# Turns of the probabilities moved directly behind the scores in two attentions of a one-core transformer kernel

## The chip, the cores and the metric

The kernel runs on one core of a Trainium2 chip. The metric is device time in microseconds (us). Three runs of the kernel before took 1641.87, 1641.92 and 1642.34 us, median 1641.92 us.

## The reference

The program computes two model blocks on one sequence of 512 tokens with width 1024, all in float32. Of these two places matter here.

The first is the attention of the first block (called **A** here): 8 heads of 64, chunks of 64 queries, each sees its own chunk and up to eight chunks to the left, with a relative bias.

```
sc = jnp.einsum('bqhd,bkhd->bhqk', q_blk, kb).astype(jnp.float32) * scale + bias
sc = jnp.where(valid[None, None, None, :], sc, -1e30)
pr = jax.nn.softmax(sc, axis=-1).astype(vb.dtype)
return jnp.einsum('bhqk,bkhd->bqhd', pr, vb)
```

The second is the sparse attention of the second block (**D** here): 8 query heads in 2 groups, and for each query block three softmaxes (over compressed keys, over selected blocks, over a window), whose outputs are weighted by gates and added:

```
o_c = jnp.einsum('bgrqn,bgnd->bgrqd', p_c, v_cmp)
o_s = jnp.einsum('bgrqn,bgqnd->bgrqd', p_s, vs_g)
o_w = jnp.einsum('bgrqn,bgnd->bgrqd', p_w, vwb)
return g_blk[..., 0:1] * o_c + g_blk[..., 1:2] * o_s + g_blk[..., 2:3] * o_w
```

Before, between and behind them stand the projections, a short convolution, a mixture of experts (96 matrices of 2 MB, streamed), an mLSTM and an HGRN layer.

## The kernel before

Every engine has one instruction stream, written out by hand in program order: `tensor` (TensorE), `vector` (VectorE), `scalar` (ScalarE), `gpsimd` and `sync` (which issues the weight DMAs). The streams meet at semaphores only. A PSUM bank is a `Fill`: TensorE waits in `fill` until the reader of the bank's previous contents has freed it (`pe.wait_ge(f.free, f.before)`), and the readers wait for `f.full`.

Both attentions are software pipelines over items. An item is a pair of heads (`hh`, u = 0 and 1) and one or two query tiles ("parts"), with at most 512 columns of scores for each head. `ITEMS_A` has 12 items (3 for each head pair), `ITEMS` has 24 (6 for each pair: one of `kind` 0 for the compressed keys, five others). The first of the five has one part, the second also, the other three have two.

In step i, TensorE does these, in this order (`softmax_a`, `softmax_d`):

1. `score(i)`: the scores of both heads, 64 rows each, in two banks of a ring of three.
2. `filling(2 * i)`: pieces of other work, to fill the time in which the other engines work on the softmax. In A a piece is a part of a projection (`seventh`, 4 matmuls, 8 in the trace, since each float32 matmul stands there twice); in D it is a part of the output projection of the mLSTM half (`out_part`, 2 matmuls, 4 in the trace).
3. `turn_probs(i - 2)`: the probabilities of item i-2 are transposed on TensorE, one bank for each head. **The ring of the turns has two banks**, `Ring(banks[3:5])`. So the first head's turns wait for the copy of the first head of item i-3, and the second head's for that of the second.
4. `filling(2 * i + 1)`.
5. `values(i - 3)`: probabilities times values.

The other engines do in step i: VectorE `lows(i)` (scores plus bias or mask, and their maximum, with a `ttr` for each part and head), `weigh(i - 1)` behind an item of kind 0, its own share of the pieces of `filling(2 * i)`, then `probs(i - 2)`, the copy of the first head's turns from PSUM, then its share of `filling(2 * i + 1)`. ScalarE does `act(..., ACT.Exp)` for each part and head of item i, and behind them `probs(i - 2)` for the second head. GpSimd scales the probabilities by the reciprocal of their sum (`weigh_a`, `weigh_d`); it signals "pa" or "pd" once for each head, and the turns wait for that.

The pieces are dealt out at build time by `softmax_slots` into two slots for each step: 4.76 pieces a step in A (2 or 3 in each slot), 0.81 in D. In D the slots `2 * i` that hold a piece, with a turn in the same step, are those of steps 2, 6, 7, 11, 12, 16, 17, 22 and 23; steps 5, 10, 15, 21, 25 and 26 hold none in either slot.

Of the kernel before, what the change touches and what calls it, by code (L numbers as in the profile page):

```python
# [186 lines left out]
def build(nc, T, out):  # L187
    with ExitStack() as ctx:
# [259 lines left out]
        ITEMS_A = list(items_a())  # L448
        NIA = len(ITEMS_A)
        ITEMS = list(items_d())  # L450
        NIT = len(ITEMS)
# [14 lines left out]
        def tensor(pe):  # L466
# [159 lines left out]
            def softmax_a(piece):  # L626
                scores, turns, out_, filler = Ring(banks[0:3]), Ring(banks[3:5]), Ring(banks[5:6]), Ring(banks[6:])

                def filling(slot):
                    now[0] = filler  # L630
                    for g, p in FILL_A[slot]:
                        piece(g, p)

                def score(it):
                    now[0] = scores
                    for u in range(2):
                        fill(("sa", it["x"] + u))
                    for part in it["parts"]:
                        c, q, nk = part["o"], part["q"], part["nk"]
                        for u in range(2):  # L640
                            f, o = F["sa", it["x"] + u], slice(64 * u, 64 * u + 64)
                            ins = mm(f.ap[:, c:c + nk], qT[o, it["hh"], q * 128:q * 128 + 128], kT[o, it["hh"], 0:nk])
                            if part is it["parts"][-1]:
                                ins.then_inc(f.full, 1)

                def turn_probs(it):
                    now[0] = turns
                    for x in (it["x"], it["x"] + 1):
                        f = fill(("pt", "A", x))
                        pe.wait_ge(S("pa"), saw("pa"))  # L650
                        for c in range(it["nk"] // 128):
                            ins = tr(f.ap[:, c * 128:c * 128 + 128], pA[x % 6][:, c * 128:c * 128 + 128])
                        ins.then_inc(f.full, 1)

                def values(it):
                    now[0] = out_
                    hh, x = it["hh"], it["x"]
                    f = fill(("yT1", hh)) if it["first"] else F["yT1", hh]
                    evacuated(("pt", "A", x), ("pt", "A", x + 1))
                    for part in it["parts"]:  # L660
                        q, o = part["q"], part["o"]
                        for c in range(q + 1):
                            for u in range(2):
                                h = 2 * hh + u
                                ins = mm(f.ap[64 * u:64 * u + 64, q * 128:q * 128 + 128], Vt[:, c, h * 64:h * 64 + 64],
                                         ptA[(x + u) % 4][:, o + c * 128:o + c * 128 + 128], c == 0, c == q)
                    if it["last"]:
                        ins.then_inc(f.full, 1)
                        pv_at["A", x] = pv_at["A", x + 1] = (f.full, f.at)
                    else:  # L670
                        ins.then_inc(S("pva"), 1)
                        pv_at["A", x] = pv_at["A", x + 1] = (S("pva"), saw("pva"))
                filling(0)
                evacuated(("qT", 2), ("qT", 3), ("w_v", "c"), ("kT", 2), ("kT", 3))
                for i in range(NIA + 3):
                    if i < NIA:
                        score(ITEMS_A[i])
                    if i:
                        filling(2 * i)
                    if 0 <= i - 2 < NIA:  # L680
                        turn_probs(ITEMS_A[i - 2])
                    filling(2 * i + 1)
                    if 0 <= i - 3 < NIA:
                        values(ITEMS_A[i - 3])
                filling(2 * (NIA + 3))
                now[0] = every

            def softmax_d(piece):
# [10 lines left out]
                def score(it):  # L699
                    hh, gg = it["hh"], it["hh"] // 2  # L700
                    now[0] = scores
                    if it["kind"] == 0:
                        fs = [fill(("skc", hh, u)) for u in range(2)]
                        for q in range(4):
                            for u, f in enumerate(fs):
                                ins = mm(f.ap[:, q * 31:q * 31 + 31], q_of(hh, u, q), kcd[64 * u:64 * u + 64, 31 * gg:31 * gg + 31])
                                if q == 3:
                                    ins.then_inc(f.full, 1)
                        return
                    for u in range(2):  # L710
                        fill(("sd", it["x"] + u))
                    for part in it["parts"]:
                        o, nk = part["o"], part["nk"]
                        for u in range(2):
                            f = F["sd", it["x"] + u]
                            ins = mm(f.ap[:, o:o + nk], q_of(hh, u, part["q"]),
                                     nkT[64 * u:64 * u + 64, gg + (2 if part["kind"] == 2 else 0), 0:nk])
                            if part is it["parts"][-1]:
                                ins.then_inc(f.full, 1)
# [43 lines left out]
                for i in range(NIT + 3):  # L763
                    if i < NIT:
                        score(ITEMS[i])
                    if i:
                        filling(2 * i)
                    if 0 <= i - 2 < NIT:
                        turn_probs(ITEMS[i - 2])
                    filling(2 * i + 1)  # L770
                    if 0 <= i - 3 < NIT:
                        values(ITEMS[i - 3])
# [635 lines left out]
        def vector(v):  # L1408
# [293 lines left out]
            def stage_a():  # L1702
# [122 lines left out]
                for i in range(NIA + 3):  # L1825
                    if i < NIA:
                        lows(ITEMS_A[i])
                    for g, p in FILL_A[2 * i]:
                        piece(g, p)
                    if 0 <= i - 2 < NIA:  # L1830
                        probs("A", ITEMS_A[i - 2]["x"], ITEMS_A[i - 2]["nk"], ptA)
                    for g, p in FILL_A[2 * i + 1]:
                        piece(g, p)
                for g, p in FILL_A[2 * (NIA + 3)]:
                    piece(g, p)
# [392 lines left out]
            def stage_d():  # L2228
# [268 lines left out]
                for i in range(NIT + 3):  # L2497
                    if i < NIT:
                        lows(ITEMS[i])
                    if 0 <= i - 1 < NIT and ITEMS[i - 1]["kind"] == 0:  # L2500
                        weigh(ITEMS[i - 1]["hh"])
                    for g, p in FILL_D[2 * i]:
                        piece(g, p)
                    if i < 4:
                        silu_z(i)
                    if 0 <= i - 2 < NIT and ITEMS[i - 2]["kind"]:
                        probs("D", ITEMS[i - 2]["x"], ITEMS[i - 2]["nk"], ptD)
                    for g, p in FILL_D[2 * i + 1]:
                        piece(g, p)
                    if 0 <= i - 3 < NIT and ITEMS[i - 3]["last"]:  # L2510
                        hh = ITEMS[i - 3]["hh"]
                        f = full("yT2", hh)
                        tt(HT[:, 4 + hh, :], f.ap, zsT[:, hh, :], MUL, f)
# [292 lines left out]
        def scalar(a):  # L2806
# [46 lines left out]
            def stage_a():  # L2853
# [33 lines left out]
                for i in range(NIA + 3):  # L2887
                    if i < NIA:
                        it = ITEMS_A[i]
                        for u in range(2):  # L2890
                            x = it["x"] + u
                            freed(("sa", x))
                            for part in it["parts"]:
                                y, low = part["y"] + u, 176 + (part["y"] + u) % 16
                                p = pA[x % 6][:, part["o"]:part["o"] + part["nk"]]
                                act(p, p, ACT.Exp, "xa", scale=-1.0, bias=small[:, low:low + 1], accum_out=sumsA[:, y:y + 1])
                    for g, p in FILL_A[2 * i]:
                        piece(g, p)
                    if 0 <= i - 2 < NIA:
                        probs("A", ITEMS_A[i - 2]["x"] + 1, ITEMS_A[i - 2]["nk"], ptA)  # L2900
                    for g, p in FILL_A[2 * i + 1]:
                        piece(g, p)
                    if 0 <= i - 3 < NIA and ITEMS_A[i - 3]["last"]:
                        hh = ITEMS_A[i - 3]["hh"]
                        f = full("yT1", hh)
                        copy(qT[:, hh, :], f.ap, f)
# [826 lines left out]
```

## Time and profile before

| what | value |
|---|---|
| median of 3 runs | 1641.92 us |
| the profiled execution's own time | 1644.87 us |
| its span, first to last instruction | 1642.9 us |
| TensorE busy | 1622.9 us (99%) |
| VectorE, ScalarE, GpSimd busy | 941.9, 391.7, 205.5 us |
| granted TensorE clock, mean | 0.999 |

The profile is of one execution, which took 2.95 us more than the median. The busy time of TensorE counts from a matmul's start to its modelled end, so matmuls overlap each other in it, and the time that one adds is read from the distance of two starts. In a timeline a row merges like instructions that follow one another: its start, its length to the last modelled end, engine, line, operation, result and operands, shapes and count. A bracket at the end tells how long the engine was idle before it and for whom. Line 483 is every matmul (`mm`), line 486 every transpose (`tr`), line 2827 every ScalarE instruction, lines 1436, 1463 and 1520 are VectorE's two-operand operation, copy and `ttr`, and 3338 and 3324 GpSimd's scaling in D and A.

### The profile page before, as it was taken

The numbers are of one execution on the slowest core, as the hardware profiler recorded it, in microseconds if no ns is written. First come the engines' busy times: TensorE is split into PE (matmuls) and PEld (weight loads), VectorE is DVE, ScalarE is ACT, GpSimd is POOL, SyncE is SP. The second block draws the span as 40 slices with busy tenths as digits, with TensorE's granted clock in tenths as the row PEclk, the third lists the DMA queues.
The fourth block names the chain that finished last, engine by engine and source line by source line (L and its number), as shares of the span: only waits on it lengthen the run. The fifth ranks groups of instructions, "written<-read, shape, count | busy, mean of one in ns | idle before, by whom it ended". The sixth has DMA issues, their size and how long they took to land.

```text
span 1642.9 us, 21311 instructions
## 1 busy us (share of the span) xinstructions
PE 1622.9 (99%) x8339; PEld 1074.5 (65%) x8339; DVE 941.9 (57%) x1577; ACT 391.7 (24%) x702; POOL 205.5 (13%) x268
## 2 busy tenths in 40 slices
PE   9999999999999999999999999999999999999999
PEld 5888888886533334333343887588866668888864
DVE  3765736683623323233233875868756757899863
ACT  3113202001210100001001122330145534644630
POOL 2333210001000000000000110101215530000000
PEclk9999999999999999999999999999999999999999
DMA  7323113234799999999999212422420020412101
GB/s 289 122 71 116 52 52 138 97 160 179 304 410 427 426 426 427 426 427 426 427 427 402 79 65 103 141 71 72 167 103 1 1 78 1 154 52 81 74 2 51
DMA packets 28359, 309.26 MB, mean 188 GB/s; under 512 B 4507, under 2 KB 4795, under 8 KB 10464
## 3 DMA queue, kind: packets, MB, share of 16 engines
q1 hardware_dynamic: 21456, 288.70, 43.2%
q0 software_dynamic: 6800, 19.16, 3.4%
q8 instruction: 68, 1.11, 0.3%
q14 instruction: 35, 0.29, 0.1%
HBM read 307.11 MB, written 4.20 MB: 189 GB/s over the span
## 4 chain that ended last, share of the span: by engine, by line
PE 80%; DVE 12%; DMA 4%; ACT 2%; issue 1%; POOL 0%; DVEq 0%; SPq 0%; ACTq 0%
PE ps L483 76%; DVE arena L1436 7%; PE ps L486 5%; DMA arena<-in_w 2%; DMA wring<-in_dense 1%; ACT arena L2827 1%; DVE arena L1447 1%; DVE wring L1436 1%; POOL small L3298 0%; DMA H<-in_x 0%; DVE arena L1463 0%; ACT L2827 0%; DVE arena L1467 0%; DVE small L1451 0%; DVE pj L1436 0%
## 5 line engine op out<-in xcount | busy, mean ns | idle before, releaser
L483 PE MATMUL ps<-arena 128*32 128x32 f32 (+9 forms) x2708 | 525.1, 377 | 2.7 <-DVE arena L1459 1.2
L483 PEld LDWEIGHTS ps<-arena 128*64 128x64 f32 (+3 forms) x2708 | 249.9, 151 | 212.3 <-issue 200.4
L483 PE MATMUL ps<-wring,arena 128*64 128x512 f32 (+3 forms) x1256 | 380.7, 528 | 0.5 <-ACT arena L2827 0.5
L1436 DVE TENSOR_TENSOR arena<-ps,arena 128x512 f32<-128x512 f32 (+2 forms) x237 | 156.1, 659 | 347.1 <-PE ps L483 190.2
L483 PE MATMUL ps<-wring 128*128 128x256 f32 x1104 | 249.5, 380 | 3.0 <-DVE arena L1436 3.0
L483 PEld LDWEIGHTS ps<-wring 128*128 128x128 f32 x1104 | 207.5, 190 | 32.7 <-DVE arena L1436 3.0
L483 PE MATMUL ps<-wring,HT 128*128 128x256 f32 (+1 forms) x704 | 219.2, 462 | 4.7 <-DVE arena L1436 3.1
L483 PEld LDWEIGHTS ps<-wring,arena 128*64 128x64 f32 (+1 forms) x1256 | 162.2, 155 | 91.5 <-issue 83.0
L2827 ACT ACTIVATE arena<-ps 128x512 f32<-128x512 f32 (+4 forms) x138 | 78.4, 568 | 584.5 <-PE ps L486 320.6
L1436 DVE TENSOR_TENSOR H<-ps,H 128x512 f32<-128x512 f32 x182 | 125.9, 692 | 89.0 <-PE ps L483 86.0
L483 PEld LDWEIGHTS ps<-wring,HT 128*128 128x128 f32 x704 | 130.9, 191 | 69.6 <-issue 54.8
L483 PE MATMUL ps<-HT,wring 128*128 128x256 f32 (+2 forms) x672 | 171.5, 416 | 0.0
L483 PEld LDWEIGHTS ps<-HT,wring 128*128 128x128 f32 (+1 forms) x672 | 123.5, 188 | 40.3 <-issue 26.2
L2827 ACT ACTIVATE arena<-arena 128x512 f32<-128x512 f32 (+7 forms) x143 | 90.0, 630 | 205.9 <-DVE arena L1436 185.5
L1463 DVE COPY arena<-ps 128x512 f32<-128x512 f32 (+4 forms) x115 | 70.6, 614 | 91.6 <-PE ps L483 71.6
L1436 DVE TENSOR_TENSOR arena<-arena 128x512 f32<-128x512 f32 (+8 forms) x179 | 112.6, 629 | 13.9 <-ACT arena L2827 3.3
L483 PE MATMUL ps<-HT,arena 128*64 128x512 f32 (+1 forms) x336 | 117.7, 503 | 0.4 <-DMA arena<-in_w 0.4
L486 PEld LDWEIGHTS ps<-con,arena 128*128 128x128 f32 (+2 forms) x713 | 84.3, 155 | 29.9 <-issue 19.7
L486 PE MATMUL ps<-con,arena 128*128 128x128 f32 (+2 forms) x713 | 94.5, 275 | 1.8 <-DVE arena L1447 1.0
L2827 ACT ACTIVATE arena<-arena,small 128x384 f32<-128x384 f32 (+3 forms) x124 | 66.5, 536 | 119.7 <-DVE small L1520 92.9
L483 PEld LDWEIGHTS ps<-HT,arena 128*64 128x64 f32 (+1 forms) x336 | 52.8, 160 | 58.6 <-issue 54.6
L483 PE MATMUL ps<-arena,wring 128*128 128x256 f32 x352 | 78.8, 379 | 0.0
(137 smaller groups left out, 1094.4 us busy)
## 6 DMA issues: line engine op xcount, KB each, us to landing
wring<-in_w SPq DMA_DIRECT2D x47, 2048.0 KB, 21.6
wring<-in_dense SPq DMA_DIRECT2D x38, 2048.0 KB, 8.3
arena<-in_w SPq DMA_DIRECT2D x35, 2048.0 KB, 19.4
HT<-in_w SPq DMA_DIRECT2D x12, 2048.0 KB, 18.2
arena<-in_rows POOLq DMA_DIRECT2D x29, 256.0 KB, 3.8
wring<-in_dense SPq DMA_DIRECT2D x2, 1024.0 KB, 5.9
H<-in_x SPq DMA_DIRECT2D x4, 512.0 KB, 7.0
arena<-in_relb POOLq DMA_DIRECT2D x8, 256.0 KB, 5.3
```

What stands on the lines that cost most here:

```text
L483: return nc.tensor.matmul(o, l, r, start=start, stop=stop, skip_group_check=True)
L486: return nc.tensor.transpose(o, i, ident[0:i.shape[0], 0:i.shape[0]])
L1436: done(nc.vector.tensor_tensor(o, a, b, op), tell)
L1447: done(nc.vector.scalar_tensor_tensor(o, a, s, b, op0, op1), tell)
L1463: done(nc.vector.tensor_copy(o, i), tell)
L2827: ins = nc.scalar.activation(o, i, fn, **k)
```

## The change

In both attentions `turn_probs(i - 2)` moves in TensorE's order from between the two slots of the step to in front of both, directly behind `score(i)`. VectorE and ScalarE do their copies of the turns in the same order. The pieces, their number and their order among themselves stay as they are, as do the rings of banks.

```diff
@@ softmax_a, tensor (softmax_d: the same lines with ITEMS and NIT)
                     if i < NIA:
                         score(ITEMS_A[i])
+                    if 0 <= i - 2 < NIA:
+                        turn_probs(ITEMS_A[i - 2])
                     if i:
                         filling(2 * i)
-                    if 0 <= i - 2 < NIA:
-                        turn_probs(ITEMS_A[i - 2])
                     filling(2 * i + 1)
@@ vector, A
                         lows(ITEMS_A[i])
-                    for g, p in FILL_A[2 * i]:
-                        piece(g, p)
                     if 0 <= i - 2 < NIA:
                         probs("A", ITEMS_A[i - 2]["x"], ITEMS_A[i - 2]["nk"], ptA)
-                    for g, p in FILL_A[2 * i + 1]:
+                    for g, p in FILL_A[2 * i] + FILL_A[2 * i + 1]:
                         piece(g, p)
@@ vector, D
                         weigh(ITEMS[i - 1]["hh"])
-                    for g, p in FILL_D[2 * i]:
-                        piece(g, p)
                     if i < 4:
                         silu_z(i)
                     if 0 <= i - 2 < NIT and ITEMS[i - 2]["kind"]:
                         probs("D", ITEMS[i - 2]["x"], ITEMS[i - 2]["nk"], ptD)
-                    for g, p in FILL_D[2 * i + 1]:
+                    for g, p in FILL_D[2 * i] + FILL_D[2 * i + 1]:
                         piece(g, p)
@@ scalar, A
-                    for g, p in FILL_A[2 * i]:
-                        piece(g, p)
                     if 0 <= i - 2 < NIA:
                         probs("A", ITEMS_A[i - 2]["x"] + 1, ITEMS_A[i - 2]["nk"], ptA)
-                    for g, p in FILL_A[2 * i + 1]:
+                    for g, p in FILL_A[2 * i] + FILL_A[2 * i + 1]:
                         piece(g, p)
```

## Rows read from the trace of the kernel before

**Rows 1.** The page: each engine's busy time, share of the span, instructions.
```profile
PE 1622.9 (99%) x8339; PEld 1074.5 (65%) x8339; DVE 941.9 (57%) x1577; ACT 391.7 (24%) x702; POOL 205.5 (13%) x268
```

**Rows 2.** Busy time by stretch (A's steps; D's steps), clock and DMA share behind.
```profile
88.00:228.00 140.00, 140.00 (x780) 115.39 (x779) 84.11 (x149) 32.76 (x84) 48.07 (x48) 1.00 0.23 83
1214.00:1318.00 104.00, 103.96 (x700) 62.34 (x700) 70.95 (x210) 55.36 (x150) 52.82 (x79) 1.00 0.09 37
```

**Rows 3.** TensorE in D, step 7: a piece, the turns, the values.
```profile
1245.40 1.98 PE L483 MATMUL ps<-wring,HT 128*128 128x512 f32 x4
1247.22 1.04 PE L486 MATMUL ps<-con,arena 128*128 128x128 f32 x8
1248.19 0.33 PE L483 MATMUL ps<-arena 128*64 128x128 f32 x2
```

**Rows 4.** TensorE in D, step 13: the turns, a piece, the values.
```profile
1272.22 1.09 PE L486 MATMUL ps<-con,arena 128*128 128x128 f32 x8
1273.15 1.88 PE L483 MATMUL ps<-wring,HT 128*128 128x512 f32 x4
1274.96 0.33 PE L483 MATMUL ps<-arena 128*64 128x128 f32 x2
```

**Rows 5.** TensorE in A, step 2: first slot, turns, second slot.
```profile
114.26 1.99 PE L483 MATMUL ps<-wring 128*128 128x256 f32 x8
...
117.82 1.04 PE L486 MATMUL ps<-con,arena 128*128 128x128 f32 x8
118.69 1.89 PE L483 MATMUL ps<-HT,arena 128*128 128x256 f32 x8
120.42 3.62 PE L483 MATMUL ps<-wring 128*128 128x256 f32 x16
```

**Rows 6.** GpSimd in A: scaling of item 0.
```profile
103.92 3.30 POOL L3324 TENSOR_SCALAR arena<-arena,small 128x512 f32<-128x512 f32 x2
```

**Rows 7.** TensorE in D: the piece behind the scores of step 6.
```profile
1240.53 1.98 PE L483 MATMUL ps<-wring,HT 128*128 128x512 f32 x4
```

**Rows 8.** ScalarE in D, step 5: the last of four exponentials, then the copy.
```profile
1240.47 0.51 ACT L2827 ACTIVATE arena<-arena,small 128x256 f32<-128x256 f32 x1
1241.18 0.60 ACT L2827 ACTIVATE arena<-ps 128x512 f32<-128x512 f32 x1
```

**Rows 9.** ScalarE's copies of the turns in steps 10, 15 and 21.
```profile
1263.13 0.60 ACT L2827 ACTIVATE arena<-ps 128x512 f32<-128x512 f32 x1
1285.12 0.60 ACT L2827 ACTIVATE arena<-ps 128x512 f32<-128x512 f32 x1
1311.79 0.60 ACT L2827 ACTIVATE arena<-ps 128x512 f32<-128x512 f32 x1
```

**Rows 10.** TensorE: the pieces behind the scores of steps 11, 16 and 22.
```profile
1262.53 1.98 PE L483 MATMUL ps<-wring,HT 128*128 128x512 f32 x4
1284.36 1.98 PE L483 MATMUL ps<-wring,HT 128*128 128x512 f32 x4
1311.02 1.98 PE L483 MATMUL ps<-wring,HT 128*128 128x512 f32 x4
```

**Rows 11.** VectorE's copies of the first head's turns, steps 5, 7 and 15.
```profile
1239.68 0.69 DVE L1463 COPY arena<-ps 128x512 f32<-128x512 f32 x1
1249.64 0.69 DVE L1463 COPY arena<-ps 128x512 f32<-128x512 f32 x1
1283.62 0.69 DVE L1463 COPY arena<-ps 128x512 f32<-128x512 f32 x1
```

**Rows 12.** TensorE: the turns of step 8 (weight load) and of step 14.
```profile
1250.38 0.36 PEld L486 LDWEIGHTS ps<-con,arena 128*64 128x64 f32 x4 [0.87 <-DVE arena L1463]
1277.05 0.63 PE L486 MATMUL ps<-con,arena 128*64 128x128 f32 x4
```

**Rows 13.** GpSimd in D: scaling of item 5, turned in step 7.
```profile
1242.28 2.16 POOL L3338 TENSOR_SCALAR arena<-arena 128x256 f32<-128x256 f32 x4
```

**Rows 14.** VectorE in A: one of the two sums of weights behind a product.
```profile
121.42 1.23 DVE L1436 TENSOR_TENSOR wring<-wring 128x1024 f32<-128x1024 f32 x1
```

More of the change, by code:

```diff
@@ L765, in softmax_d @@
                         score(ITEMS[i])
+                    if 0 <= i - 2 < NIT:
+                        turn_probs(ITEMS[i - 2])
                     if i:
                         filling(2 * i)
-                    if 0 <= i - 2 < NIT:
-                        turn_probs(ITEMS[i - 2])
                     filling(2 * i + 1)
```

## The prediction

> **What bounds the kernel now.** I read the page first, then the busy time by stretch, then timelines of single steps, one engine at a time. The page shows TensorE busy for 99% of the span and nothing else above 57% [rows 1]. Its busy time counts modelled ends, so it proves little alone; the stretches say more. In A's steps TensorE is busy for 140.00 of 140.00 us, in D's for 103.96 of 104.00, at full granted clock (1.00, the 2.4 GHz level) [rows 2]. The sum of both stages is thus the sum of the distances between TensorE's starts, and work of the other engines is hidden. A reordering can save only what a change from one kind of matmul to the next costs, and can lose wherever a wait that a piece covers today comes to light. Each stage ends before the next can begin, so what TensorE loses or gains in either I pass on to the end in full (an estimate; the expert stage in between streams weights from slots that TensorE itself frees, so it shifts with it).
>
> **The change, part by part.**
>
> Removed or added instructions: none, on any engine. No DMA is issued in the moved step; GpSimd's and the DMA queue's streams are unchanged.
>
> *The order on TensorE.* The turns now follow the scores (64 rows) and not a piece (128 rows). The trace holds both orders of the same work in D. In step 7, a piece of four 512-column matmuls and then eight turns take 1245.40 to 1248.19, 2.79 us [rows 3]. In step 13, where the piece was dealt to the second slot, eight turns and then the piece take 1272.22 to 1274.96, 2.74 us [rows 4]; both follow scores of 512 columns and precede values. The new order saves 0.05 us each time. In A the pieces are 256 columns wide, and the cost of coming from the scores shows there as well: the first 16 matmuls behind them take 114.26 to 117.82, 3.56 us, against 1.73 us for 8 (118.69 to 120.42, the next slot's first half; two such make 3.46) [rows 5]. I take 0.05 us there too. A has 12 steps with both a piece in the first slot and a turn (i = 2 to 13), D has 9. Sum: 21 x 0.05 = 1.05 us saved. The bounds are 0 (the difference of two rounded readings) and 21 x 0.10 = 2.1 us, if the turns hid the whole cost of leaving the scores.
>
> The Trainium skill (TensorE: Matmul & The Clock Gate, Step-by-step: what each phase is for) says that the load of the next tile's weights is pulled ahead beside the running matmul, if the row groups don't conflict or it goes to the background buffer. Taken at its word, a change between 64 and 128 rows costs nothing and the 1.05 us fall away; the rows above differ by 0.05 us in D and 0.10 us in A, so I go by the rows. The result by the rule stands among the rivals.
>
> *The cover of the turns' inputs.* The turns of item i-2 need GpSimd's scaling. They now start earlier by the first slot: 3.56 us in A's step 2, 1.82 us in D (1245.40 to 1247.22) [rows 3, 5]. In A the scaling of item 0 ends at 107.22, and the turns move from 117.82 to 114.26: 7.0 us to spare [rows 5, 6]; read in the same way, none of the eleven later items has less. In D, item 5 is scaled at 1244.44; its turns move from 1247.22 to 1245.40, and those of the second head, which that time holds for, stand 0.44 us later (half of eight turns): 1.4 us to spare [rows 3, 13]. So no wait for GpSimd, but thin cover in D. If it went, the excess over 1.4 us would be paid in steps 7, 12, 17 and 23, whose turns are of items with two parts (in 6 and 11 the wait of the next paragraph lies over it).
>
> *The cover of the turns' banks.* This is where I expect the change to be decided. The turns have two banks; those of the next step need the copies of this step's. What stands between two turns is, before, the second slot of step i, values, scores and the first slot of step i+1; after, both slots of step i, values and scores. Summed over all steps that is the same, but the pieces sit elsewhere, and four steps with a turn in the next have no piece at all: 5, 10, 15 and 21. (In step 25 too, but there no turn follows.) Each is followed by a step whose first slot holds a piece, which today covers. After the change it is: turns, values, scores, turns.
>
> Step 5: the item has two parts, so ScalarE does four exponentials (the last starts at 1240.47) before it copies the second head's turns, 1241.18 to 1241.78 [rows 8]. VectorE's copy of the first head ends at 1240.37 [rows 11]. The next scores end at 1240.53, where the piece starts now [rows 7]. The new turns start there; the first head's bank is free since 0.16 us. The second head's would start 0.50 us later, at 1241.03: 0.06 us that the first turn behind scores takes longer (0.93 from 1272.22 to 1273.15 against 8 x 0.109, the steady distance, which is 0.87 us for eight from 117.82 to 118.69) and four turns, 0.44 [rows 4, 5]. Its bank is free at 1241.78, and TensorE needs 0.05 to 0.06 us to notice: the copy that ends at 1250.33 lets the weight load of step 8 go at 1250.38 [rows 11, 12]. Wait: 1241.84 - 1241.03 = 0.81 us. These steps' exponentials start when VectorE's first maximum is there, which hangs on the scores, not on the order of the pieces, so the copy can't come sooner.
>
> The other three in the same way, with the copy's end [rows 9] and the end of the scores [rows 10]: 1263.73 + 0.06 - 1263.03 = 0.76; 1285.72 + 0.06 - 1284.86 = 0.92; 1312.39 + 0.06 - 1311.52 = 0.93. VectorE's copy of step 15, the tightest, ends at 1284.31 [rows 11], 0.05 us before the scores do: first head free, just. Sum of the four: 3.42 us. The bounds: nothing, if ScalarE's copy came ahead of its exponentials; and 4 x (0.86 + 0.70) = 6.2 us, if a fifth exponential with its gap stood before it (0.70 us is the distance of its copy from the fourth's start, 1240.47 to 1241.18). I take the middle value, since all its terms are rows of the very steps.
>
> *What else is queued behind.* Behind the waiting turns on TensorE stand the piece, the values and the next scores; they shift by the wait, and so does all work of the other engines that hangs on scores. Each of the steps 6, 11, 16 and 22 has its piece behind the turns now, so a late copy there finds 1.8 us more cover than today: the wait isn't passed on as a second one.
>
> *A wait that goes.* Step 8 has the turns behind values and scores today, and the weight load waits for VectorE's copy until 1250.38 [rows 12]; that copy stood behind the step's piece on VectorE. The values and scores before it start at 1248.19 and the turns at 1250.39, 2.20 us later; the same work takes 2.09 us from 1274.96 to 1277.05, one round of items on [rows 3, 4, 12]. TensorE loses 0.11 us. After, the copy comes before the piece, and a piece of TensorE stands in between: 0.11 us saved.
>
> *VectorE and ScalarE in A.* VectorE gets its copy earlier, then up to five pieces in one run. TensorE needs the bank of a product again one product (3.5 us) later; VectorE's longest share behind one product is one addition and two sums of weights of 1.23 us each [rows 14], of which only the addition, the first, frees the bank. It is busy for 84 of 140 us [rows 2]. I cost it at nothing; if that cover went it would be a few tenths in each of four or five projections, 2 us at most.
>
> Sum: 3.42 - 0.11 - 1.05 = +2.26 us. The profiled execution would go from 1644.87 to 1647.1 us. It lay 2.95 us above the median shown, so I forecast 1641.92 + 2.3 = 1644.2 us.
>
> **The rivals.**
>
> *Not slower: the banks come free in time.* If the second head's copy is there when the turns want it at all four places, what is left is the saving, -1.16 us: 1640.8 us. For it: today turns follow each other with no piece between them into steps 8, 13, 18 and 24, and of those only step 8's wait, 0.11 us. Against it: items with two parts and so four exponentials stand in all four steps, and their rows put the copy 0.8 us too late. It decides at 0.8 us.
>
> *Slower by more than can be told from noise: GpSimd's scaling comes late in D.* Place: the turns of steps 7, 12, 17 and 23, with 1.4 us of cover left. If items of two parts are scaled 2 us later against their scores than now, each costs 0.6 us: 2.4 us on top of the forecast, 1646.6 us. It decides from 1.4 us. For it: GpSimd takes 2.16 us to scale such an item [rows 13], and two follow each other. Against it: it is busy in half of the stretch [rows 2], and ScalarE, which feeds it, gets its copy no later than now.
>
> *The switch is free* (from the rows 3 and 4 alone, if their difference is rounding): 3.42 - 0.11 = +3.3, 1645.2 us. That is the result by the skill's rule above.
>
> *A's run of five pieces makes TensorE wait for VectorE*: +2 us on top, 1646.2 us. Against it: the first piece in the run is over when VectorE has done its maxima and its copy.
>
> **How the numbers follow.** Forecast (between 1642.8 and 1645.1 us) 0.62; not slower 0.14; switch free 0.08; GpSimd late 0.08; A's run 0.05; something faster by more than all this 0.03. A measurement of this kernel tells about 0.2%, 3.3 us, from no change: faster is below 1638.6, slower above 1645.2. The forecast and the first rival lie inside; "switch free" lies on the bound and is split; the last two rivals lie above. Faster 0.03, same 0.80, slower 0.17. Range for 8 in 10: from 1640.8 (the first rival) to 1646.8 us (just above GpSimd late); the likeliest case's own is 1642.8 to 1645.1 us.
>
> **What would show it.** In the changed kernel the turns of steps 6, 11, 16 and 22 have a gap of 0.8 to 0.9 us between the first four and the last four, put down to ScalarE line 2827, and no other wait in either stage; A is shorter by about 0.6 us, D longer by 2.9 us. The wait of step 8 is gone. Wrong it is if there is no such gap, if a wait for GpSimd stands before a turn in D, or if A's stretch grows.

## The result, and the profile after

The changed kernel takes 1644.77 us (median of 18 runs, 1643.57 to 1647.4), the kernel before 1642.29 us (18 runs beside them, 1641.23 to 1643.37). The ratio is 1.0016, with a 95% interval of 1.001 to 1.0023: slower by 2.5 us. The forecast was 1644.2 us against a median of 1641.92, so +2.3. The difference is 0.16%, inside the 0.2% within which the prediction called a result "same".

The page of the changed kernel has the same instructions and nearly the same busy times as [rows 1]:

```profile
PE 1622.1 (99%) x8339; PEld 1074.5 (65%) x8339; DVE 941.5 (57%) x1577; ACT 391.7 (24%) x702; POOL 207.7 (13%) x268
```

Its span is 1642.4 us, shorter than the 1642.9 of the kernel before, though the kernel is slower. The two profiled executions differ where the change does nothing: in the one of before TensorE has a granted clock of 0.50 (the 1.2 GHz level) from 11.21 to 14.62, its first row below. The changed kernel shows 1.00 there, and by the start of the 150th matmul it is 2.11 us ahead. The spans can't be compared for 2.5 us.

```profile
11.21:14.62 3.41, 3.41 (x5) 1.35 (x4) 1.50 (x2) 1.44 (x3) 2.52 (x4) 0.50 1.03 348
```

So each stage is measured inside itself, between two landmarks that exist in both kernels. In A: from the sixteen turns ahead of the steps to the last sixteen values. The kernel before, TensorE:

```profile
93.73 1.91 PE L486 MATMUL ps<-con,arena 128*128 128x128 f32 x16
...
241.02 1.09 PE L483 MATMUL ps<-arena 128*64 128x128 f32 x16
```

The changed kernel:

```profile
91.62 1.91 PE L486 MATMUL ps<-con,arena 128*128 128x128 f32 x16
...
238.35 1.09 PE L483 MATMUL ps<-arena 128*64 128x128 f32 x16
```

147.29 us became 146.73: A is 0.56 shorter (0.57 between the starts of the 450th and the 1350th matmul, the measure used for all kernels below). In D, from the scores of step 1 to the pieces behind the last values, before:

```profile
1217.10 1.13 PE L483 MATMUL ps<-arena 64*128 64x512 f32 x4
...
1326.51 3.70 PE L483 MATMUL ps<-wring,HT 128*128 128x512 f32 x8
```

and after:

```profile
1213.47 1.13 PE L483 MATMUL ps<-arena 64*128 64x512 f32 x4
...
1326.03 4.56 PE L483 MATMUL ps<-wring,HT 128*128 128x512 f32 x10
```

109.41 us became 112.56: D is 3.15 longer (also between the 5550th and the 6450th matmul). 3.15 - 0.57 = +2.58 us, and the medians differ by 2.48. Between the stages the changed execution is 0.95 us shorter; two executions of one and the same kernel (the copy-first one below) differ there by 1.6 us, so that is no part of the change. The stretch behind D differs by 0.02. The stage differences themselves repeat: the same two executions agree to 0.01 us in A and in D. The stages by stretch, as in [rows 2] and at the same work:

```profile
85.90:225.90 140.00, 140.00 (x783) 115.86 (x782) 83.81 (x149) 32.76 (x84) 50.08 (x48) 1.00 0.23 83
1210.40:1314.40 104.00, 101.26 (x687) 59.68 (x686) 69.20 (x202) 54.29 (x146) 50.93 (x75) 1.00 0.09 36
```

TensorE was busy for 103.96 of 104 us in D; now 101.26: 2.7 us of idle time, at full clock, and thirteen matmuls fewer in the same time. In A nothing is idle. The waits of TensorE (us in total, times, longest) have one new row, the second:

```profile
PE ps L483 <- DVE arena L1436: 8.3, 11, 1.3
PE ps L486 <- ACT arena L2823: 2.7, 4, 0.8
PE ps L483 <- ACT HT L2823: 1.7, 2, 1.4
```

L2823 is what L2827 was in the kernel before. TensorE's turns of steps 6, 11, 16 and 22 (first four, second four, the piece behind):

```profile
1236.83 0.66 PE L486 MATMUL ps<-con,arena 128*128 128x128 f32 x4
1238.14 0.66 PE L486 MATMUL ps<-con,arena 128*128 128x128 f32 x4 [0.64 <-ACT arena L2823]
1238.63 0.59 PE L483 MATMUL ps<-wring,HT 128*128 128x512 f32 x1
...
1259.49 0.66 PE L486 MATMUL ps<-con,arena 128*128 128x128 f32 x4
1260.75 0.66 PE L486 MATMUL ps<-con,arena 128*128 128x128 f32 x4 [0.60 <-ACT arena L2823]
1261.24 1.02 PE L483 MATMUL ps<-wring,HT 128*128 128x512 f32 x2
...
1282.06 0.66 PE L486 MATMUL ps<-con,arena 128*128 128x128 f32 x4
1283.47 0.66 PE L486 MATMUL ps<-con,arena 128*128 128x128 f32 x4 [0.75 <-ACT arena L2823]
1283.96 1.02 PE L483 MATMUL ps<-wring,HT 128*128 128x512 f32 x2
...
1309.62 0.66 PE L486 MATMUL ps<-con,arena 128*128 128x128 f32 x4
1311.03 0.66 PE L486 MATMUL ps<-con,arena 128*128 128x128 f32 x4 [0.75 <-ACT arena L2823]
1311.52 1.02 PE L483 MATMUL ps<-wring,HT 128*128 128x512 f32 x2
```

and what they wait for, on ScalarE:

```profile
1236.77 0.51 ACT L2823 ACTIVATE arena<-arena,small 128x256 f32<-128x256 f32 x1
1237.49 0.60 ACT L2823 ACTIVATE arena<-ps 128x512 f32<-128x512 f32 x1
```

The first four turns go at 1236.83, the second four only at 1238.14, 0.05 us behind the end of the copy (1238.09), as [rows 8, 11, 12] let one expect. The idle time in brackets counts from the modelled end of the turns before; the loss is read from the distances of the starts.

A fifth, small wait of this kind stands in step 24. TensorE's list doesn't show it, since the modelled end of the turns before covers it; ScalarE's copy and the weight load behind it do:

```profile
1319.13 0.60 ACT L2823 ACTIVATE arena<-ps 128x512 f32<-128x512 f32 x1
1319.78 0.42 PEld L486 LDWEIGHTS ps<-con,arena 128*128 128x128 f32 x4 [0.17 <-ACT arena L2823]
```

The eight turns take 1.08 us there (1319.19 to 1320.27) and not 0.93, a loss of 0.16 before rounding. The kernel before has this wait too, smaller, with 1.04 us, a loss of 0.11:

```profile
1319.71 1.21 PE L486 MATMUL ps<-con,arena 128*128 128x128 f32 x8
1320.75 1.88 PE L483 MATMUL ps<-wring,HT 128*128 128x512 f32 x4
```

### The profile page after: what moved, and what is told of

It reads as the page before. It is cut to its first block, busy times and chain, and to the rows that moved or that the text cites. A ratio compares the mean times of both kernels' runs of the same rounds, so it can differ in the third digit from the quotient of the medians.

```text
span 1642.4 us, 21311 instructions
## 1 busy us (share of the span) xinstructions
PE 1622.1 (99%) x8339; PEld 1074.5 (65%) x8339; DVE 941.5 (57%) x1577; ACT 391.7 (24%) x702; POOL 207.7 (13%) x268
## 4 chain that ended last, share of the span: by engine, by line
PE 84%; DVE 12%; ACT 3%; issue 1%; POOL 1%; DVEq 0%; ACTq 0%
PE ps L483 79%; DVE arena L1436 7%; PE ps L486 5%; ACT arena L2823 2%; DVE arena L1447 1%; DVE wring L1436 1%; POOL small L3292 1%; DVE arena L1463 0%; ACT L2823 0%; DVE arena L1467 0%; DVE small L1451 0%; DVE pj L1436 0%; DVE arena L1441 0%; DVE arena L1520 0%; DVE H L1436 0%
## 5 line engine op out<-in xcount | busy, mean ns | idle before, releaser
L2823 ACT ACTIVATE arena<-ps 128x512 f32<-128x512 f32 (+4 forms) x138 | 78.4, 568 | 575.7 <-PE ps L486 295.1
L2823 ACT ACTIVATE arena<-arena 128x512 f32<-128x512 f32 (+7 forms) x143 | 90.0, 630 | 206.6 <-DVE arena L1436 186.2
L2823 ACT ACTIVATE arena<-arena,small 128x384 f32<-128x384 f32 (+3 forms) x124 | 66.5, 536 | 128.3 <-DVE small L1520 101.4
```

The lines of the kernel that those rows point to most:

```text
L2823: ins = nc.scalar.activation(o, i, fn, **k)
```

## The experiments

"Step" and "turns" are used as before. A wait is the idle time that the trace puts ahead of an instruction, its cost the distance of the starts over that of an undisturbed run. "D +3.15" is the difference of the D stage from the kernel before. The kernels with a ratio are timed against the kernel before, with a 95% interval; the others ran once, and their stages are read from the trace.

**One half of the change at a time.** The first kernel has only A's lines of the diff, the second only D's.

```diff
@@ A only (tensor; with it vector's and scalar's lines of A)
+                    if 0 <= i - 2 < NIA:
+                        turn_probs(ITEMS_A[i - 2])
                     if i:
                         filling(2 * i)
@@ D only (tensor; with it vector's lines of D)
+                    if 0 <= i - 2 < NIT:
+                        turn_probs(ITEMS[i - 2])
                     if i:
                         filling(2 * i)
```

> The new order in attention A alone; D as before. My theory: A gains 12 x 0.05 us from coming to the turns and not to a piece behind the scores, 0.57 us over its steps in the trace, and no wait appears: 1641.7 us, ratio 0.9997. The rival 'A's run of five pieces makes TensorE wait for VectorE' wants A's stretch longer by up to 2 us. The rival 'the switch is free' wants 0.00 in A.

> The new order in attention D alone; A as before. My theory: four waits of TensorE for ScalarE's copy (0.81, 0.76, 0.92, 0.91 us), each with 0.06 us for starting again, less 0.43 us of switches and 0.11 us of the old wait: D's stretch longer by 3.1 us, the whole 1645.4 us, ratio 1.0019. If something else than the order in D made the kernel slower, it comes out within 1 us of the kernel before.

A only: 1641.65 us (11 runs), ratio 0.9997 (0.9988 to 1.0006), A -0.57, D 0.00. D only: 1645.54 us (11 runs), ratio 1.002 (1.0011 to 1.003), A 0.00, D +3.14. The halves add up, and all of the loss is D's. A's -0.57 over its 12 steps is 0.048 us each.

**What the four waits are for.** Rival theories: the second head's probabilities come late (from GpSimd), or its bank does. Three banks for the turns, taken from the pieces of D (which then have one), leave the probabilities as they are:

```diff
-  scores, turns, out_, filler = Ring(banks[5:]), Ring(banks[3:5]), Ring(banks[0:1]), Ring(banks[1:3])
+  scores, turns, out_, filler = Ring(banks[5:]), Ring(banks[2:5]), Ring(banks[0:1]), Ring(banks[1:2])
```

> The change, and in D the turns get a third bank, taken from the two of the pieces. ScalarE and VectorE work in the same order at the same time. If the waits are for the two banks, all four go; if they are for the probabilities (exponentials or scaling late), they stay, since a bank doesn't bring those. The pieces' single bank costs one wait of about 0.9 us in step 1, where the third of three pieces wants it behind VectorE's maxima and weighing. D's stretch against the kernel before: +0.4 us by my theory, +4 us by the rival.

One execution, 1645.36 us; A -0.57, D +1.67 where +0.4 was expected. All four waits are gone, and step 24's with them; step 6 of this kernel:

```profile
1241.83 1.10 PE L486 MATMUL ps<-con,arena 128*128 128x128 f32 x8
1242.76 0.59 PE L483 MATMUL ps<-wring,HT 128*128 128x512 f32 x1
```

Eight turns in 0.93 us: it was the bank. The price is elsewhere, and was expected once and came twice. Pieces that share one bank wait for VectorE to add up the last one, and VectorE comes to it behind other work:

```profile
1218.12 3.67 PE L483 MATMUL ps<-wring,HT 128*128 128x512 f32 x8 [0.84 <-DVE H L1436]
1222.99 1.95 PE L483 MATMUL ps<-wring,HT 128*128 128x512 f32 x4 [1.20 <-DVE H L1436]
```

```profile
1221.30 0.75 DVE L1447 SCALAR_TENSOR_TENSOR arena<-arena,pcl 128x512 f32<-128x512 f32 x1
1222.15 0.69 DVE L1436 TENSOR_TENSOR H<-ps,H 128x512 f32<-128x512 f32 x1
```

The two cost 0.92 and 1.37 us, and -0.64 (the stage with no waits, below) + 2.3 gives the +1.67.

**The cause, taken away on ScalarE.** If the bank is late because ScalarE copies behind its exponentials, then copying ahead of them frees it: in the trace the eight turns are long over when the last exponential starts.

```diff
@@ scalar, D's loop, step i
+                    if i in (3, 4):
+                        a.wait_ge(S("zg"), 2 * i - 4)
+                    if 0 <= i - 2 < NIT:
+                        ...            # the copy of the second head's turns, unchanged
                     ...                # the exponentials of item i
-                    if i in (3, 4):
-                        a.wait_ge(S("zg"), 2 * i - 4)
-                    if 0 <= i - 2 < NIT:
-                        ...
```

> The change as it is, and in D ScalarE copies the second head's turns ahead of the step's exponentials, not behind them. My theory: the banks are then free some 1.7 us behind the scores, where the next turns want them after 3.5; all four waits go, D's stretch is 0.5 us shorter than in the kernel before, the whole 1641.2 us, ratio 0.9993. The exponentials start 0.65 us later, inside the 1.4 us of cover of GpSimd's scaling. If the waits came from the scaling or from VectorE's copy, they stay: 1644.8 us. If the cover of the scaling is less than 0.65 us, new waits for GpSimd stand in steps 7, 12, 17 and 23.

1641.14 us (11 runs), ratio 0.9992 (0.9983 to 1.0001); A -0.57, D -0.64. The same kernel, timed a second time:

> The change with ScalarE's copy ahead of the exponentials once more, for a narrower interval: D's stretch -0.6 us, A's -0.6 us against the kernel before, ratio 0.9993.

1640.86 us (11 runs), ratio 0.9993 (0.9984 to 1.0002), the same -0.57 and -0.64. Its ScalarE in step 5, and TensorE in step 6:

```profile
1235.68 0.60 ACT L2823 ACTIVATE arena<-ps 128x512 f32<-128x512 f32 x1 [1.53 <-PE ps L486]
1236.38 0.51 ACT L2823 ACTIVATE arena<-arena,small 128x256 f32<-128x256 f32 x1
```

```profile
1237.61 1.10 PE L486 MATMUL ps<-con,arena 128*128 128x128 f32 x8
```

ScalarE now waits 1.53 us for the turns, time in which it used to do exponentials, and nobody behind it suffers. With the waits gone the change is worth what its reordering saves, and in D the waits of steps 8 and 24, 0.11 us each, are gone with them. This version beats the changed kernel by 3.8 us by the trace, by 3.6 and 3.9 by the medians. Against the kernel before it is 1.2 us faster by the trace (0.57 + 0.64) and 1.0 and 1.3 by the medians; both intervals just reach 1, so the times alone don't prove it.

**Is it the new copying order, or both together?** The same edit in the kernel before:

> The kernel before, with one edit: in D ScalarE copies the turns ahead of the step's exponentials. The turns still stand behind the first piece. My theory: it brings nothing here, since no bank was waited for but VectorE's once; it can cost, because the exponentials of a step with a first piece now wait 2.9 us for the copy, so that GpSimd's scaling ends some 2 us later against its scores, with 3.2 us of cover in that order: D's stretch 0.0 to +0.6 us, the whole 1642.2 to 1642.8 us. If copying first is worth something by itself, D's stretch falls here as it did with the change (-0.6).

A miss: 1643.81 us (11 runs), ratio 1.0011 (1.0002 to 1.002), D +1.47 where 0 to 0.6 was expected. In the old order the turns stand behind a piece, so ScalarE's exponentials, now behind the copy, start that much later, and GpSimd, which scales them, too:

```profile
1311.85 0.60 ACT L2827 ACTIVATE arena<-ps 128x512 f32<-128x512 f32 x1 [1.46 <-PE ps L486]
1312.54 0.62 ACT L2827 ACTIVATE arena<-arena,small 128x384 f32<-128x384 f32 x1
```

```profile
1318.89 0.63 PE L486 MATMUL ps<-con,arena 128*128 128x128 f32 x4 [0.44 <-POOL arena L3338]
...
1323.48 0.63 PE L486 MATMUL ps<-con,arena 128*128 128x128 f32 x4 [0.44 <-POOL arena L3338]
```

These two, in steps 24 and 25, cost about 0.6 us each, and the first four turns of both steps another 0.2. The expectation took 3.2 us of cover for the scaling everywhere. Before the turns of these two steps stand neither scores nor a piece, and in the kernel before the scaling ends only 1.3 and 0.7 us ahead of them. Turning early and copying early help only together: alone the one costs 3.1 us in D and the other 1.5; together they gain 0.6.

**The other cure: a piece back in the gap.** The four steps before a wait (5, 10, 15, 21) have no piece at all. Give each one from a neighbour, with the order of the pieces unchanged:

```diff
+    todo, counts = [x for s in FILL_D for x in s], [len(s) for s in FILL_D]
+    for a_, b_ in ((7, 5), (8, 10), (13, 15), (20, 21)):
+        counts[2 * a_ if counts[2 * a_] else 2 * a_ + 1] -= 1
+        counts[2 * b_ + 1] += 1
+    FILL_D = [[todo.pop(0) for _ in range(n)] for n in counts]
```

> The change as it is, and D's pieces dealt otherwise: those of steps 7, 8, 13 and 20 go to steps 5, 10, 15 and 21, so that the steps without a piece are ones whose items take two exponentials and not four. My theory: the copy is there in time everywhere, the four waits go, D's stretch 0.5 us shorter than before, the whole 1641.2 us, ratio 0.9993. If it is the mere lack of a piece that costs (any two turns with only values and scores between them), four waits of about the same size appear at steps 8, 9, 14 and 21: 1644.8 us.

1643.78 us (11 runs), ratio 1.0011 (1.0002 to 1.002), D +2.29: the four waits are gone, but 1641.2 was expected. The steps that gave a piece away (7, 13) now lay the same trap, one engine further: the next step's turns wait for VectorE's copy of the first head, which stands behind its maxima and a weighing. VectorE, then TensorE in step 8:

```profile
1248.42 0.42 DVE L1441 TENSOR_TENSOR arena<-arena,small 128x248 f32<-128x248 f32 x1
1248.97 0.69 DVE L1468 COPY arena<-ps 128x512 f32<-128x512 f32 x1
```

```profile
1249.72 0.63 PE L491 MATMUL ps<-con,arena 128*64 128x128 f32 x4 [1.01 <-DVE arena L1468]
```

Two of these cost 1.08 us each, and 0.24 and 0.39 us were lost in steps 9 and 21; with step 24's 0.16 that is 2.95 over the -0.64 of the stage without waits, which makes 2.31 against the 2.29 measured. So the pieces were dealt again, from the steps right behind the waits, (6, 5), (12, 10), (18, 15), (24, 21), in the same lines:

> The change, with D's pieces dealt a third way: those of steps 6, 12, 18 and 24 go to steps 5, 10, 15 and 21. The last dealing met two waits of 1.1 us at steps 8 and 14, for VectorE's copy, which stood behind the maxima and the weighing of a compressed item (copy ended 1249.66, 4.1 us behind the scores of step 7, wanted after 3.1). Theory, refined: a step without a piece costs the amount by which the later copy's end exceeds 3.1 us (first head) or 3.5 us (second) behind its scores. In steps 6, 12 and 18 VectorE's copy ends 2.9 and ScalarE's 3.3 us behind them, both in time. So no wait in D above 0.1 us, D's stretch 0.5 us shorter than in the kernel before, the whole 1641.2 us, ratio 0.9993. If any step without a piece costs, three waits at steps 7, 13 and 19: some 1644 us.

1641.42 us (11 runs), ratio 0.9998 (0.9989 to 1.0007), D +0.16. Of the waits at banks only step 24's small one is left. One new wait came instead, for GpSimd, in step 25, where step 24 lost its piece:

```profile
1321.88 0.63 PE L491 MATMUL ps<-con,arena 128*128 128x128 f32 x4
1322.95 0.63 PE L491 MATMUL ps<-con,arena 128*128 128x128 f32 x4 [0.44 <-POOL arena L3337]
```

It costs 0.6 us where no wait above 0.1 was expected: the scaling has less to spare at D's end than in its middle (in the changed kernel it ends at 1322.39, and the turns of the second head stand at 1323.55, so 1.2 us, less than the 1.8 of the piece that step 24 gave away).

**How much cover is there for GpSimd?** The second rival turned on 1.4 us. Here GpSimd's power of the sums (1.0 us) is done twice in each weighing, so that each scaling comes that much later and TensorE's stream stays the same:

```diff
                 nc.gpsimd.tensor_tensor(rcp..., ALU.pow).then_inc(S("g"), 1)
                 g.wait_ge(S("g"), told("g"))
+                nc.gpsimd.tensor_tensor(rcp..., ALU.pow).then_inc(S("g"), 1)
+                g.wait_ge(S("g"), told("g"))
```

> The change, and GpSimd takes the reciprocals of each item in D twice (1.0 us, with its semaphore 1.1 us more an item, nothing else changed). The cover of the scaling was worked out as 1.4 us; if that is right, the 1.1 us cost nothing: D's stretch +3.1 us against the kernel before, as in the changed kernel. If GpSimd decides the turns' times, each of the 12 items with two parts adds to the waits: +3 us and more on top, and the waits are put down to GpSimd.

One execution, 1644.16 us; D +3.18. GpSimd has the second copy of the operation, and the waits of TensorE are still those for ScalarE:

```profile
1237.25 1.02 POOL L3325 TENSOR_TENSOR arena<-arena,con 128x4 f32<-128x4 f32 x1 [0.46 <-ACT arena L2823]
1238.35 1.01 POOL L3328 TENSOR_TENSOR arena<-arena,con 128x4 f32<-128x4 f32 x1
```

```profile
PE ps L486 <- ACT arena L2823: 2.8, 4, 0.8
```

1.1 us later on GpSimd costs 0.03 us: in the changed kernel the cover is at least that nearly everywhere. That it is 1.4 us no run shows, and at D's end it is 1.2 (above).

**Which head's bank is late?** If the wait is for the bank that ScalarE frees, and ScalarE copies the first head's turns instead of the second's, the wait must move to the front of the eight turns and grow by the 0.44 us of four turns and the 0.06.

```diff
@@ vector
-                        probs("D", ITEMS[i - 2]["x"], ITEMS[i - 2]["nk"], ptD)
+                        probs("D", ITEMS[i - 2]["x"] + 1, ITEMS[i - 2]["nk"], ptD)
@@ scalar
-                            probs("D", it["x"] + 1, it["nk"], ptD)
+                            probs("D", it["x"], it["nk"], ptD)
```

> The change, and in D VectorE copies the second head's turns and ScalarE the first head's. If TensorE waits for the bank that ScalarE frees, the wait moves from the middle of the turns to before the first and grows by the 0.5 us of the first four: 1.3, 1.3, 1.4 and 1.4 us, sum 5.4; less 0.24 us, as nothing starts again in the middle. D's stretch against the kernel before: +4.9 us (+3.1 unswapped). If it waits for both copies or for something else, it stays at +3.1.

One execution, 1648.96 us, D +7.05. The waits moved to the first turn and cost 1.30, 1.25, 1.41 and 1.41 us, sum 5.37. The fifth in the row, 0.59, is step 24's, moved and grown in the same way; the expectation of +4.9 had left it out:

```profile
PE ps L486 <- ACT arena L2823: 5.6, 5, 1.3
```

With the -0.64 of the stage without waits that makes 5.3 of the 7.05. The rest is the clock: right behind the first wait TensorE's granted clock fell to the 1.2 GHz level, its share being 0.53 over this stretch:

```profile
1238.80:1242.40 3.60, 3.54 (x11) 2.52 (x12) 1.46 (x4) 1.02 (x3) 2.56 (x5) 0.53 0.00 0
```

```profile
1238.86 1.97 PE L486 MATMUL ps<-con,arena 128*128 128x128 f32 x8 [1.23 <-ACT arena L2823]
```

The eight turns take 1.97 us busy instead of 1.09. To see whether the wait does that each time, the kernel ran once more:

> The swapped heads once more. In the first look the granted clock fell to 1.2 GHz for 3.4 us behind the first of the four waits, which are 1.2 to 1.4 us long. If such a wait at that place brings it down each time, D's stretch is +7 us again with a dip behind step 6's wait; if it comes and goes, D's stretch is +5.5 us without a dip (5.4 of waits, 0.6 more for a new one in step 24 or 25, less 0.5).

One execution, 1647.11 us, D +5.40, with the same waits and the full clock throughout:

```profile
1238.58 1.09 PE L486 MATMUL ps<-con,arena 128*128 128x128 f32 x8 [1.23 <-ACT arena L2823]
```

The place and the size of the waits are confirmed. The fall of the clock came in one of two executions and is no part of the change.

## Why the prediction was right, point by point

*The four waits* (predicted 0.81, 0.76, 0.92, 0.93 us, sum 3.42). From the first turn to the piece behind the eighth, steps 6, 11, 16 and 22 take 1.80, 1.75, 1.90 and 1.90 us (1236.83 to 1238.63, and so on) instead of the 0.93 of [rows 4]: 3.63 us. The second four turns start 1.31, 1.26, 1.41 and 1.41 us behind the first; less the 0.50 of the prediction, the waits are 0.81, 0.76, 0.91 and 0.91 us, sum 3.39. The mechanism and each size hold. Not counted was the restart: the second four take 0.49 us up to the piece, where 0.93 - 0.50 = 0.43 was left for them; 4 x 0.06 = 0.24. The waits are shown by three runs, each in another way: three banks remove them, copying first removes them, and swapping the heads moves them and adds what it should. The Trainium skill (Perfetto Trace Analysis, Optimization Strategy) says that a gap that repeats on the engine which should be saturated can mean too little PSUM; the third bank bears that out, and copying first shows that two banks suffice if the one is freed in time.

*The wait of step 8* (predicted -0.11). Gone: from the scores of step 8 to those of step 9 it is 4.36 us instead of 4.47. TensorE there, the turns 0.52 us behind the start of two matmuls of the scores, with no idle time:

```profile
1246.83 0.60 PE L483 MATMUL ps<-arena 64*128 64x512 f32 x2
1247.35 0.63 PE L486 MATMUL ps<-con,arena 128*64 128x128 f32 x4
```

*The saving of 0.05 us per step* (predicted 21 x 0.05). A alone gives 0.57 / 12 = 0.048 where only this counts. For D's nine steps the same would be 0.43. The Trainium skill (TensorE: Matmul & The Clock Gate, Step-by-step: what each phase is for) says that the load of the next weights is pulled ahead if the row groups don't conflict or it goes to the background buffer. The prediction's reading of it, that a change between 64 and 128 rows is then free, would have left A unchanged; A's 0.57 us speaks against that reading. It does not speak against the page, since no run shows whether these loads meet its condition. Where in the array the 0.05 us goes no run shows either.

*The sum for D* (predicted +2.9). 3.63 - 0.43 - 0.11 = 3.09 against 3.15 measured. The remainder is step 24. The prediction said that of today's turns without a piece ahead only those of step 8 wait, and that no wait but the four would stand in either stage; both were wrong by this small wait, which grew from 0.11 to 0.16. With it the sum is 3.14. It closes from the other side as well: measured from the version without waits the changed kernel's cost 3.15 + 0.64 = 3.79, which is 3.63 + 0.16, and the -0.64 is 0.43 of reordering and 0.11 each for steps 8 and 24. Of the forecast, the restart (0.24) was missing and step 24 (0.05) overlooked, both small. That +2.3 lies so near the measured +2.5 is not luck, as the four waits that make it up came one by one in size and place.

*GpSimd's cover* (1.4 us, no wait). No wait for it in the changed kernel, and 1.1 us more on it cost 0.03 us. Its end is close, though: where a step near D's end lost a piece, it was late by 0.6 us. *A's run of pieces* costs nothing: no idle time in A, and no wait for VectorE there. *No second wait behind the first:* none in the trace behind any of the four. *Not slower* (the first rival) was right in its condition and wrong in fact: it is what the kernel does when the copy comes first, 1641.14 and 1640.86 us, where the rival said 1640.8.

## What to carry to other kernels

A block of filler between two uses of a small ring of banks covers the slower of the two copies that free them; before moving it, compare for every step, not on average, the end of that copy with the start of the next use, and look first at the steps that have no filler. When such a distance is shortened, put the copy that frees the bank ahead of the longer work on the engine that does both, and check who waits for that longer work: this pair of edits gained where each alone lost. Filler is dealt by what the other engines do in a step, and a piece taken from a neighbour takes away a cover there as well.

## What the hardware showed beside this

A wait in the middle of a run of turns costs 0.06 us beyond its length, each of five times (step 24's too). TensorE's list of waits showed four of the five; the one of 0.10 us stood only in the weight loads' timeline. The granted clock fell to the 1.2 GHz level for 3.41 us, from 1238.87, behind an idle time of 1.23 us in one execution, and did not in the next with the same idle time; it cost 7.05 - 5.40 = 1.65 us. In the profiled execution of the kernel before, a stretch of the same 3.41 us fell near the start. One such stretch is as large as most of the differences studied here, so a difference of 2 us between two spans should be placed in the timeline before it is explained.
